# Loading each cached page into every fourth partition, four tokens in a row

## The reference, cut to what matters

```python
kp = k_pool[page_table].reshape(bsz, -1, H_B, 2, DB)
vp = v_pool[page_table].reshape(bsz, -1, H_B, 2 * DB)
s_past = jnp.einsum('bqhmd,bkhmd->bhmqk', qf, kp)
s = jnp.concatenate([s_past, s_new], axis=-1) * (DB ** -0.5)
p = jax.nn.softmax(s, axis=-1); wts = p[:, :, 0] - lam * p[:, :, 1]
return (jnp.einsum('bhqk,bkhe->bqhe', wts[..., :past], vp)
        + jnp.einsum('bhqk,bkhe->bqhe', wts[..., past:], v))
```

## Time and profile before

| what | value |
|---|---|
| median of 3 runs (lowest to highest) | 5597.93 us (5591.04 to 5605.55) |
| span of the profiled execution | 5596.8 us |
| busy in the span: PE, DVE, ACT, POOL | 91%, 41%, 27%, 13% |
| mean granted TensorE clock | 0.942 |
| bytes moved by the DMA engines | 487.21 MB |
| cached pages: issues and size | 1024 of 128 KB, 134 MB |

### The profile page before, as it was taken

One profiled execution on the slowest core, in us unless ns is written; L12 is line 12 of the kernel. 1 busy time (PEld: TensorE's weight loads), 2 busy tenths in 40 slices (PEclk: granted clock), 3 DMA queues, 4 the chain that ended last, 5 costly groups with the idle time before them and its releaser, 6 DMA issues.

```text
span 5596.8 us, 91764 instructions
## 1 busy us (share of the span) xinstructions
PE 5101.1 (91%) x35274; PEld 3196.3 (57%) x35274; DVE 2314.3 (41%) x5351; ACT 1495.2 (27%) x3427; POOL 715.9 (13%) x935
## 2 busy tenths in 40 slices
PE   8978889886868868999999999989999899999998
PEld 5644445444545555666667666665666555557554
DVE  1145655562445424544444444245342443312222
ACT  3224444442223212222222222132121321112112
POOL 0011121212223301111011110110101101010000
PEclk9989999998889876999999999999999999997999
DMA  3101111014768642122231222322233222242232
GB/s 97 54 29 37 36 34 36 31 36 123 219 210 250 208 112 63 53 74 85 84 99 52 75 82 86 92 58 81 80 89 90 62 71 66 82 131 71 87 89 71
DMA packets 747025, 487.21 MB, mean 87 GB/s; under 512 B 78007, under 2 KB 728247, under 8 KB 746556
## 3 DMA queue, kind: packets, MB, share of 16 engines
q1 hardware_dynamic: 673822, 384.50, 24.1%
q10 hardware_dynamic: 60480, 63.27, 3.4%
q0 software_dynamic: 12288, 33.57, 1.9%
HBM read 432.12 MB, written 49.09 MB: 86 GB/s over the span
## 4 chain that ended last, share of the span: by engine, by line
PE 55%; DVE 3%; ACT 1%; issue 1%; DMA 0%; POOL 0%; SPq 0%; DVEq 0%; ACTq 0%; POOLq 0%
PE s_f_b L3390 28%; PE s_f_b L3450 11%; PE s_bank L2387 2%; PE s_bank L2380 2%; PE s_f_b L3441 2%; PE s_bank L2386 2%; PE s_f_b L3431 1%; PE s_f_b L3395 1%; PE s_bank L2502 1%; PE s_f_b L3411 0%; DVE s_r_o L2658 0%; PE s_bank L3778 0%; PE s_bank L2571 0%; PE s_bank L2969 0%; PE s_bank L2951 0%
## 5 line engine op out<-in xcount | busy, mean ns | idle before, releaser
L3390 PE MATMUL s_f_b<-s_arena 128*128 128x384 f32 (+2 forms) x4480 | 1635.9, 520 | 17.6 <-PEq L123 9.3
L3390 PEld LDWEIGHTS s_f_b<-s_arena 128*128 128x128 f32 x4480 | 840.3, 192 | 690.9 <-issue 466.9
L543 PE MATMUL s_p_acc<-s_hT,s_p_W 128*128 128x416 f32 x1600 | 630.8, 542 | 6.8 <-DMA s_p_W<-in_w_in_dram 6.8
L3450 PE MATMUL s_f_b<-s_f_a,s_arena 128*128 128x384 f32 (+2 forms) x1760 | 636.4, 518 | 0.0
L3450 PEld LDWEIGHTS s_f_b<-s_f_a,s_arena 128*128 128x128 f32 x1760 | 331.1, 191 | 266.8 <-issue 180.5
L543 PEld LDWEIGHTS s_p_acc<-s_hT,s_p_W 128*128 128x128 f32 x1600 | 303.0, 198 | 292.6 <-issue 276.5
L3657 DVE TENSOR_TENSOR s_f_xT<-s_f_xT,s_f_b 128x384 f32<-128x384 f32 (+2 forms) x160 | 93.7, 587 | 531.5 <-PE s_f_b L3450 457.8
L3678 POOL TENSOR_TENSOR s_f_ex<-s_f_ex,s_f_mix 128x384 f32<-128x384 f32 (+2 forms) x105 | 112.7, 1073 | 1429.7 <-ACT s_f_mix L3480 1429.4
L897 ACT ACTIVATE s_prob<-s_s_ps,s_ntop 128x512 f32<-128x512 f32 (+3 forms) x320 | 196.5, 620 | 360.3 <-DVE s_ntop L948 360.3
L3527 ACT ACTIVATE s_f_raw<-s_f_b 128x384 f32<-128x384 f32 (+2 forms) x110 | 56.9, 517 | 731.4 <-PE s_f_b L3390 731.4
L945 DVE TENSOR_REDUCE s_ntop<-s_s_ps 128x2 f32<-128x1024 f32 (+3 forms) x160 | 169.7, 1061 | 46.4 <-PE s_s_ps L843 44.2
(11 more groups left out here) (797 smaller groups left out, 7808.7 us busy)
## 6 DMA issues: line engine op xcount, KB each, us to landing
s_arena<-in_ffn_w_in_dram SPq DMA_DIRECT2D x220, 512.0 KB, 3.9
s_K<-in_cache_diff_k_dram SPq DMA_DIRECT2D x384, 128.0 KB, 3.1
s_arena<-in_ffn_w_out_dram SPq DMA_DIRECT2D x80, 448.0 KB, 3.8
s_arena<-in_cache_diff_v_dram POOLq DMA_DIRECT2D x256, 128.0 KB, 3.7
s_arena<-in_cache_diff_v_dram ACTq DMA_DIRECT2D x192, 128.0 KB, 3.5
cols_t<-s_p_out ACTq DMA_DIRECT2D x100, 208.0 KB, 1.9
s_arena<-in_w_out_dram SPq DMA_DIRECT2D x40, 512.0 KB, 4.3
s_arena<-in_ffn_w_out_dram SPq DMA_DIRECT2D x40, 512.0 KB, 4.1
```

Source lines behind the costliest of these rows:

```text
L543: mm = pe.matmul(self.acc[n % 2][:, 0:CH], self.W[:, u, k, :], self.hT[:, k, c * CH:(c + 1) * CH], start=(k == 0), stop=(k == KD - 1))
L3390: mm = pe.matmul(bank(u)[:, 0:G], w[:, k, :], h[:, k, 0:G], start=(k == 0), stop=(k == KD - 1 and kind != "op"))
L3450: mm = pe.matmul(bank(u)[:, 0:G], w[:, k, :], a[:, f % NA, 0:G], start=(k == 0), stop=(k == len(part) - 1))
```

## The change

Each of the five places that load a page gets another pattern on both sides. `four` reads the page as 32 rows of 4 tokens (4 KB in one piece), and `part` writes them to the partitions i, i+4, i+8, ... of page i's group, each row into the 4 KB that the group has in that partition. So page i now lies in every fourth partition, and partition 4r+i holds the tokens 4r to 4r+3 of page i. The four pages of a group together fill the same 128 partitions and the same bytes as before. The order of the tokens is changed alike for K and V. No other instruction, wait, ring or queue is changed.

```diff
--- before.py
+++ after.py
@@ -1109,6 +1109,12 @@
     on_act = lambda job: job[2] % 2 == 0
     nth = {job: sum(on_act(o) == on_act(job) for o in flip_order[:n + 1]) for job, n in place.items()}
 
+    def four(page):
+        return page.rearrange("a (r t) h d -> r (a t h d)", t=4)
+
+    def part(ring, slot, i):
+        return ring[i::4, slot, :, :].rearrange("p t n -> p (t n)")
+
     def page_of(eng, g, i):
         return bass.ds(eng.value_load(table[0:1, g * 4 + i:g * 4 + i + 1], min_val=0, max_val=n_pool - 1), 1)
 
@@ -1117,13 +1123,13 @@
             if g >= KG:
                 sp.wait_ge(flipped, place[("k", g - KG, 1)] + 1)
             for i in range(3):
-                sp.dma_start(K[:, g % KG, i, :], kp[page_of(sp, g, i)].rearrange("a p h d -> p (a h d)"))\
+                sp.dma_start(part(K, g % KG, i), four(kp[page_of(sp, g, i)]))\
                   .then_inc(k_in[g % KG], 16)
 
         def v_page(g):
             if g >= VG:
                 sp.wait_ge(pv, (g - VG) // 4 + 1)
-            sp.dma_start(V_[:, g % VG, 2, :], vp[page_of(sp, g, 2)].rearrange("a p h d -> p (a h d)"))\
+            sp.dma_start(part(V_, g % VG, 2), four(vp[page_of(sp, g, 2)]))\
               .then_inc(v_sp[g % VG], 16)
 
         sp.dma_start(table[:, :], pr.i["page_table"].rearrange("(a b) n -> a (b n)", a=1)).then_inc(init, 16)
@@ -1154,7 +1160,7 @@
                 if g >= VG:
                     pool.wait_ge(pv, (g - VG) // 4 + 1)
                 for i in range(2):
-                    pool.dma_start(V_[:, g % VG, i, :], vp[page_of(pool, g, i)].rearrange("a p h d -> p (a h d)"))\
+                    pool.dma_start(part(V_, g % VG, i), four(vp[page_of(pool, g, i)]))\
                         .then_inc(v_in[g % VG], 16)
             yield
         yield
@@ -1292,14 +1298,14 @@
         def k_page(g):
             if g >= KG:
                 act.wait_ge(flipped, place[("k", g - KG, 1)] + 1)
-            act.dma_start(K[:, g % KG, 3, :], kp[page_of(act, g, 3)].rearrange("a p h d -> p (a h d)"))\
+            act.dma_start(part(K, g % KG, 3), four(kp[page_of(act, g, 3)]))\
                .then_inc(k_act[g % KG], 16)
 
         def v_pages(g):
             if g >= VG:
                 act.wait_ge(pv, (g - VG) // 4 + 1)
             for i in (2, 3) if g % 2 else (3,):
-                act.dma_start(V_[:, g % VG, i, :], vp[page_of(act, g, i)].rearrange("a p h d -> p (a h d)"))\
+                act.dma_start(part(V_, g % VG, i), four(vp[page_of(act, g, i)]))\
                    .then_inc(v_act[g % VG], 16)
 
         def turn(job):
```

## The result

Over 10 runs of each kernel, the time went from 5596.56 us (5585.04 to 5605.55) to 5622.36 us (5609.93 to 5644.61). These are medians, with the lowest and the highest run; they differ by 25.8 us, 0.46%. The ratio over the runs is 1.0054 with an interval of 1.0039 to 1.007, so the change makes the kernel about half a per cent slower. The forecast was 5588 us. The profiled span is 5618.4 us, against 5596.8.

What follows compares the result with a forecast made beforehand. In the cached-page stage neither TensorE nor DMA is full; late page landings cost TensorE 35.4 us of waits. V 8, K 2.5 and clock 2.5 us made 13, less 3 given back: -10 us, so 5588 us, range 5560 to 5620.

Steps and rivals of the forecast that it cites:

- Issue: DMA instructions of page loads: zero change for SyncE's and ScalarE's 768; GpSimd saves 0 to 536 ns each, taken as zero.
- rival 3: Page writes to 32 partitions, not 128, move at down to half rate; 5620 to 5680 us, likeliest 5625; chance 0.12.
- rival 4: Dearer page issues on SyncE set the stage's pace from +0.3 us; +17 to +40 us; chance 0.06 with anything unseen.
- SyncE's pace limits K early in the stage: SyncE's six K issues take 6.27 us, 1.04 each, mostly reading page numbers; this stays and limits early K supply.
- Transfer: Page stage: 4 KB rows raise a busy DMA engine's rate by 0 to 18%, taken as 8%.
- The second effect: With packets equal to GpSimd's, ScalarE's pages lose less time behind GpSimd's; counted together with the rate gain.
- 0.9 us for a V page and 0.5 for a K page: Landing time saved per late page by rate and equal packets together; bounds 0 and the least landing, 1.9 us.
- the sum: Page stage: V waits 8 us, K waits 2.5, clock 2.5, together 13; 3 given back, so -10 us.
- GpSimd: GpSimd's 256 page issues: between 0 and 536 ns saved each, 0 to 137 us of GpSimd, taken as zero.
- What would show it: Signs in the profile after: 673,000 packets, issues of 338 and 349 ns, median landings 2.8 to 3.3 us, shorter V and K waits.

Runs made afterwards that it cites:

- adj32: The changed kernel with page i on the 32 adjacent partitions from 32 i on, not every fourth; 5621.79 us, ratio 1.0054 to the kernel before.
- step2: The changed kernel with 64 rows of 2 KB on every second partition, two pages side by side; 5623.15 us, ratio 1.0048 to the kernel before.
- long_both: The kernel before with the prepared-DMA mark taken off its 768 SyncE and ScalarE page loads, data movement untouched; 5623.55 us, ratio 1.0056.
- move_b: The kernel before with the V page that SyncE issues given to GpSimd; 5586.23 us, ratio 0.9985.

## Why the prediction was wrong

The forecast was no change or slightly faster, with 0.18 on slower, and it came out slower. The time, 5622, is 2 us beyond the top of the range.

**The step that failed is "Issue", "I take zero for the 768 pages of SyncE and ScalarE".** It measured +0.134 us on SyncE and +0.139 on ScalarE. The row count was rightly left out of the price: the earlier trace rows say so, and `adj32` with its 32 rows (321 ns for the 338 of 128 rows) and `step2` with 64 (475 ns for the 472 of 32) bear it out to 20 ns. What doesn't follow is the second half of the sentence, that both patterns cost the same because they "remain two-dimensional". Both loads of the earlier trace rows write to adjacent partitions, and the change doesn't. They compared a property that hardly matters and held the one that did. The prediction noted "No row here has a load on every fourth partition", but only in rival 3, about transfers; the issue was left without a bound from both sides, though the same engine's other loads in that stage (L4130 and L4132, from 431 to 631 ns in the median of a group) offered an upper one of +0.1 to +0.3 us. With it rival 4 would have had to weigh more than 0.06.

**Rival 4 had the mechanism, and its threshold was too high.** It set +0.3 us as the point from which SyncE sets the pace, from 3.6 us of issues to a group and a slot of 4.65. The first was read too low: it divided the 6.27 us of six issues by six, but the last of them stands there with its own 0.34 us only, and six issues without a wait stand 3.87 / 3.5 = 1.1 us apart. So SyncE needs 3.87 us to a group. The second was an average over the stage: between the 8th and the 24th group one took 4.2 us, and that was SyncE's own pace, with the small loads in its queue, since it waited only 0.8 us for a ring place up to group 32. There was no room in that stretch, and every 0.134 us was too much. The price it gave, 17 to 40 us, holds what was measured, 24 us of the stage. All K waits of the earlier trace rows fell before group 24, which the list by windows would have shown: it was the sign that SyncE was late there already. The prediction's sentence that SyncE's pace limits K early in the stage had this bound in words, but no price was put on it.

**Transfer** was too high, 8% for a measured 3 to 4%, near the bound that the 4 KB rows gave. The second effect, that equal packets let ScalarE's pages lose less behind GpSimd's, can't be seen in the landings, 3.2 and 3.6 us in the median before and after. So the 0.9 us for a V page and 0.5 for a K page didn't come, and with them -8, -2.5 and -2.5 us of the sum. `long_both`, which has the dear issues without the new rows, is as slow as the change; that bounds what all transfer effects brought together at about 0.2%, of either sign. That alone would still allow the 10 us of the forecast; the unchanged landings speak against them.

**GpSimd.** 526 for 536 ns, inside the bounds, 256 x 0.01 = 3 us, without an effect that shows.

**Rival 3** was right to be named and right to be doubted for this pattern: it shows with adjacent partitions (`adj32`) and not with every fourth.

**What would show it.** The packets came as forecast. The line "DMA instructions of 338 and 349 ns as before (else rival 4)" named the right sign, and it decided. That the other stages keep their times within 2 us was too strict: 7.5 us between the two profiles is within the scatter of single ones.

**What stays open.** How the loss divides between the two engines, and between K and V pages: each half alone gives more than half; that their waits overlap is likely, not shown. Whether ScalarE's part goes through its copies or through its page loads. No 64 adjacent partitions ran.

## What to carry to other kernels

A DMA whose transfer is hidden still costs its issue, and the issue's price can hang on the form of the on-chip side: check whether a row of the trace has the new form exactly, and else bound the issue from above by the engine's dearest loads. An engine's lead must be read by stretches, since waits summed over a stage (51.0 us here) can hide a quarter of it with no lead at all. When a queue sets the pace, try first to move an issue to an engine with room: one in seven took the K waits from 11.3 to 6.3 us (`move_b`), though the 0.15% of the time that it seemed to bring is not certain.

## What the runs showed of the hardware

- A load of 128 KB with its page number in a register took SyncE 338 ns and ScalarE 349 with all 128 partitions, 321 and 327 with 32 adjacent ones, and 472 to 475 and 488 to 491 with every second or fourth partition, or with the mark of the prepared DMA taken off. GpSimd: 536, 489, and 526 with every fourth.
- The same 4 KB rows ran at 19.8 GB/s per engine on every fourth partition and 15.9 on 32 adjacent ones, and a K page landed in 3.2 and 4.4 us in the median.
- Rows of 4 KB in place of 1 KB raised the rate of a busy engine by only 3 to 4% (19.3 to 19.8 and 18.3 to 19.0 GB/s), and left the median landings of K and V at 3.2 and 3.6 us.
- Reading one page number took SyncE 0.27 us, reading three with one load 0.67, so that one load for three saves little.
- The Trainium skill, "DMA: Bandwidth & Descriptors", section "Issuing engines are not separate DMA queues", says that issuing from several engines saves only the sequencer's own time, usually small beside the DMA. The issue is small here too, 0.34 to 0.47 us on SyncE beside a landing of 3.2. Its growth by 0.13 us was still enough for the whole of the loss (`long_both`), for up to group 32 SyncE's queue had no room.
